# A two-layer attention trunk: the per-head factors of its output stages go through DRAM rows instead of TensorE turns, and the first tile is split by halves

## The chip, the core and the metric

The kernel runs on one core of a Trainium2 chip. The metric is the time of one execution on the device in microseconds; the time of a kernel is the median of its runs. The traces are of one profiled execution each.

## The reference, cut to what matters

```python
# per layer: attention heads o (SEQ x D), gate g, output projection, residual, norm
mixed = jnp.concatenate([a_out * jax.nn.silu(ag), b_out * jax.nn.silu(bg)], axis=-1)   # layer 0
y = mixed @ w_out_even[i]
...
y = (c_out * jax.nn.silu(cg)) @ w_out_odd[i]                                            # layer 1
...
x = x + y
return rms_norm(x, final_g)
```

SEQ is 2048, D is 1024, everything is float32. The attention outputs are left without their softmax denominators (heads of B and C) and without their RMS factor (heads of A). So an output stage computes, for each token and channel, `o * g * f`, where the factor `f` depends only on the token and on the head that the channel belongs to; then it multiplies by the output weights, adds the residual and norms.

## The kernel before, in words

There are two output stages, one per layer, both written by `output()` (L2144). The first ("stage 0") follows `small_attn` and precedes the projection of layer 1; the second ("stage 1") follows `band_attn` and is the end of the program. Each stage handles 16 tiles of 128 tokens. Everything is laid out with channels on the partitions: 8 chunks of 128 channels (two heads of 64 channels each; in stage 0 the first 4 chunks are one A head each) by 128 tokens.

For tile t:

- POOL *widens* (L1593, L1594): the factors lie with tokens on the partitions and one column per head. POOL copies each column over the channels of its head, into `post_wide`. Tiles 0 and 1 are widened at the end of the attention stage, tiles 2 to 15 inside the output stage, each as soon as its buffer of two is free.
- TensorE *spreads* (`spreads(t)`, L2294): 16 transposes of 64x128 turn `post_wide` so that channels are on the partitions, into PSUM `spread`.
- VectorE *splits* (`split(t)`): `gated = g * spread` (L2254), `mix = o * gated` (L2257); ScalarE rounds `m_hi = mix` (L2223); VectorE forms `m_lo = mix - m_hi` (L2259).
- TensorE multiplies (L2309): for each half of 512 output columns, 8 chunks by three products (hi by hi, lo by hi, hi by lo), 48 matmuls of 128x512 per tile.
- VectorE adds the residual per half (`y`, L2275); ScalarE squares and sums (L2232) and takes the root (L2234); VectorE forms the inverse with one step of refinement (L79 to L82, L2277, L2279) and writes `n` (L2281).
- SyncE issues the loads and stores: x of tile t+2 (L2194) once y of tile t is done, the y store (L2208, stage 0 only), the n store (L2210), and, at tiles 0, 4 and 8, the next block of 512 tokens of o and g, 2 MB each (L2189). The first block is loaded tile by tile during the attention stage (L1588, 512 KB each in runs of 512 bytes). All of these use one queue. (The loads of q and k in the first attention stage, L1260 to L1262 in `diff_attn`, go to 64 partitions each, in runs of 2 KB; around 640 us they are what the DMA engines carry.)

The order on TensorE is written out: `spreads(0)`; then for each t: `spreads(t+1)`, wait for `m_lo` of t, 48 matmuls. On VectorE it is `split(0)`, a wait for the gain vector, then for each t: `split(t+1)`, y of t in two halves, norm of t. Two buffers exist for `post_wide`, `m_hi`, `m_lo`, x, y and n, and four PSUM banks for the accumulators, so y of tile t waits for the y and n stores of tile t-2.

Of the kernel before, what the change touches and what calls it, by code (L numbers as in the profile page):

```python
# [20 lines left out]
F32 = mybir.dt.float32  # L21
F32R = mybir.dt.float32r
ALU = mybir.AluOpType
ACT = mybir.ActivationFunctionType
AX = mybir.AxisListType

P = 128
SEQ, D = 2048, 1024
KC = D // P
TILES = SEQ // P  # L30
BLK = 512
NBLK = SEQ // BLK
TPB = BLK // P
HD = 64
EPS = 1e-6
SCALE = HD ** -0.5
A_HEADS, B_HEADS, B_GROUP, C_HEADS = 4, 8, 4, 16
# [7 lines left out]
ROW = 384  # L45
# [2098 lines left out]
def output(nc, before, name, keep, scr, x_dram, w_hi, w_lo, y_dram, norm_dram, gain_dram, post, rms=None, after=None):  # L2144


    with ExitStack() as ctx:
        st = Stage(nc, ctx, name, before)
        o_sb, g_sb = post.o, post.g
        m_hi = st.sb("m_hi", [P, 2, KC, P], F32R)  # L2150
        m_lo = st.sb("m_lo", [P, 2, KC, P], F32R)
        gated, mix = st.sb("gated", [P, KC, P]), st.sb("mix", [P, KC, P])
        x_sb = st.sb("x", [P, 2, D])
        y_sb = st.sb("y", [P, 2, D])
        n_sb = st.sb("n", [P, 2, D])
        gain = st.sb("gain", [P, D])
        ssq, mean, root, inv = (st.sb(x, [P, TILES]) for x in ("ssq", "mean", "root", "inv"))
        acc = [st.ps(f"acc{i}", [P, BLK]) for i in range(4)]
        junk = st.ps("junk", [P, D])
        spread = st.ps("spread", [P, 2, KC * HD])  # L2160
        spread_tokens = spread[:, :, :].rearrange("p r (c t) -> p c r t", t=HD)
        spread_done, scaled = (st.sem(x) for x in ("spread_done", "scaled"))
        gain_loaded = st.sem("gain_loaded")
        blk_loaded, x_loaded, y_stored, n_stored = (st.sems(x, 2) for x in ("blk_loaded", "x_loaded", "y_stored", "n_stored"))
        mixed, hi_done, lo_done, mm_done, y_done = (st.sem(x) for x in ("mixed", "hi_done", "lo_done", "mm_done", "y_done"))
        sq_done, mean_done, root_done, inv_done, normed = (st.sem(x) for x in ("sq_done", "mean_done", "root_done", "inv_done", "normed"))
        ot = scr["ot"].rearrange("(c p) t -> p c t", p=P)
        gt = scr["gt"].rearrange("(c p) t -> p c t", p=P)
        x_v, y_v, n_v = (None if d is None else d.rearrange("(t p) d -> t p d", p=P) for d in (x_dram, y_dram, norm_dram))
        block = ctx.enter_context(nc.Block())  # L2170

        @block.gpsimd
        def _(pool):
            st.clear_before(pool)
            if after is not None:
                after.load_weights(pool)
            for t in range(2, TILES):
                pool.wait_ge(spread_done, t - 1)
                post.widen(t, rms)

        @block.sync
        def _(sp):
            def load_block(b):
                if b >= 2:
                    sp.wait_ge(mixed, TPB * (b - 1))
                    sp.wait_ge(lo_done, TPB * (b - 1))
                sp.wait_ge(post.stored[b], 16 * (post.heads // 2))
                for buf, part in ((o_sb, ot), (g_sb, gt)):
                    sp.dma_start(buf[b % 2][:, :, :], part[:, :, b * BLK:(b + 1) * BLK]).then_inc(blk_loaded[b % 2], 16)  # L2189

            def load_x(t):
                if t >= 2:
                    sp.wait_ge(y_done, 2 * (t - 1))
                sp.dma_start(x_sb[:, t % 2, :], x_v[t]).then_inc(x_loaded[t % 2], 16)  # L2194

            load_x(0)
            load_x(1)
            sp.dma_start(gain[:, :], gain_dram.partition_broadcast(P)).then_inc(gain_loaded, 16)
            for t in range(TILES):
                if t + 2 < TILES:  # L2200
                    load_x(t + 2)
                if t == 0:
                    load_block(1)
                elif t % TPB == 0 and t // TPB + 1 < NBLK:
                    load_block(t // TPB + 1)
                if y_v is not None:
                    sp.wait_ge(y_done, 2 * (t + 1))
                    sp.dma_start(y_v[t], y_sb[:, t % 2, :]).then_inc(y_stored[t % 2], 16)  # L2208
                sp.wait_ge(normed, t + 1)
                sp.dma_start(n_v[t], n_sb[:, t % 2, :]).then_inc(n_stored[t % 2], 16)  # L2210
                if after is not None and t == TPB + 2:
                    sp.wait_ge(n_stored[0], 16 * (TPB // 2 + 1))
                    after.load_tiles(sp, n_v)
            for s in n_stored + (y_stored if y_v is not None else []):
                sp.wait_ge(s, 16 * TILES // 2)

        @block.scalar
        def _(act):
            def hi(t):
                act.wait_ge(mixed, t + 1)  # L2220
                if t >= 2:
                    act.wait_ge(mm_done, 2 * (t - 1))
                nc.scalar.activation(m_hi[:, t % 2, :, :], mix[:, :, :], ACT.Copy).then_inc(hi_done, 1)  # L2223

            hi(0)
            for t in range(TILES):
                if t + 1 < TILES:
                    hi(t + 1)
                act.wait_ge(y_done, 2 * (t + 1))
                if t >= 1:  # L2230
                    act.wait_ge(sq_done, t)
                nc.scalar.activation(junk[:, :], y_sb[:, t % 2, :], ACT.Square, accum_out=ssq[:, t:t + 1]).then_inc(sq_done, 1)  # L2232
                act.wait_ge(mean_done, t + 1)
                nc.scalar.activation(root[:, t:t + 1], mean[:, t:t + 1], ACT.Sqrt).then_inc(root_done, 1)  # L2234

        @block.vector
        def _(dve):
# [8 lines left out]
            def split(t):  # L2246
                b = t // TPB
                if b == 0:
                    dve.wait_ge(post.tile_loaded[t], 32)
                elif t % TPB == 0:  # L2250
                    dve.wait_ge(blk_loaded[b % 2], 32 * ((b + 1) // 2))
                tokens = slice(t % TPB * P, (t % TPB + 1) * P)
                dve.wait_ge(spread_done, t + 1)
                nc.vector.tensor_tensor(gated[:, :, :].rearrange("p c (r t) -> p c r t", t=HD), g_sb[b % 2][:, :, tokens].rearrange("p c (r t) -> p c r t", t=HD),  # L2254
                                        spread_tokens, ALU.mult).then_inc(scaled, 1)
                dve.wait_ge(scaled, t + 1)
                nc.vector.tensor_tensor(mix[:, :, :], o_sb[b % 2][:, :, tokens], gated[:, :, :], ALU.mult).then_inc(mixed, 1)  # L2257
                dve.wait_ge(hi_done, t + 1)
                nc.vector.tensor_tensor(m_lo[:, t % 2, :, :], mix[:, :, :], m_hi[:, t % 2, :, :].bitcast(F32), ALU.subtract).then_inc(lo_done, 1)  # L2259

            split(0)
            dve.wait_ge(gain_loaded, 16)
# [21 lines left out]
        @block.tensor  # L2284
        def _(pe):
            def spreads(t):

                if t >= 1:
                    pe.wait_ge(scaled, t)
                pe.wait_ge(post.widened, (t + 1) * (2 if post.earlier else 1))  # L2290
                for c in range(KC):
                    for r in range(2):
                        rows = slice(r * HD, (r + 1) * HD)
                        last = nc.tensor.transpose(spread[:, r, c * HD:(c + 1) * HD], post.wide[rows, t % 2, c, :], keep["ident"][rows, rows])  # L2294
                last.then_inc(spread_done, 1)

            spreads(0)
            for t in range(TILES):
                if t + 1 < TILES:
                    spreads(t + 1)  # L2300
                pe.wait_ge(lo_done, t + 1)
                for half in range(2):
                    u = 2 * t + half
                    if u >= 4:
                        pe.wait_ge(y_done, u - 3)
                    step = 0
                    for c in range(KC):
                        for mt, wt in ((m_hi, w_hi), (m_lo, w_hi), (m_hi, w_lo)):
                            last = nc.tensor.matmul(acc[u % 4][:, :], mt[:, t % 2, c, :], wt[:, c, half * BLK:(half + 1) * BLK],  # L2309
                                                    start=step == 0, stop=step == 3 * KC - 1)  # L2310
                            step += 1
                    last.then_inc(mm_done, 1)
# [10 lines left out]
def trunk(nc, src, out):  # L2323
# [1 line left out]
        ("qh", (2 * C_W, SEQ), F32), ("ql", (2 * C_W, SEQ), F32), ("gt", (D, SEQ), F32), ("ot", (D, SEQ), F32),  # L2325
        ("v0_a", (SEQ, A_W), F32), ("v0_b", (B_KV // HD, P, TILES, HD), F32), ("v1", (C_HEADS, P, TILES, HD), F32), ("x1", (SEQ, D), F32), ("xn", (SEQ, D), F32),
        ("row_a", (A_HEADS, REL), F32), ("row_b", (B_HEADS, REL), F32), ("row_c", (C_HEADS, REL), F32),
        ("skew_a", (A_HEADS, P, ROW), F32), ("skew_b", (B_HEADS, P, ROW), F32), ("skew_c", (C_HEADS, P, ROW), F32))}
    with ExitStack() as ctx:
        keep = {name: ctx.enter_context(nc.sbuf_tensor(f"keep_{name}", shape, F32)) for name, shape in (  # L2330
            ("ident", [P, P]), ("sink", [P, B_HEADS]), ("sub_g", [P, 1]), ("nlam", [P, 1]))}

        w_loaded = [ctx.enter_context(nc.semaphore(f"w_loaded{i}")) for i in range(6)]
        x, norm_g = src["x"][0], src["norm_g"]
# [59 lines left out]
```

## Time and profile before

| | us |
|---|---|
| median of 3 runs | 2559.77 (2558.9 to 2565.64) |
| the profiled execution's own time | 2567.35 |
| its span | 2565.5 |
| stage 0, from the first spread to the last n store | about 1079 to 1282 |
| stage 1, the same | about 2363 to 2565.5 |

The span is what the trace covers; the execution's own time is 1.85 us more. Busy time of TensorE is the share of time with a matmul under way; matmuls are pipelined, so the interval between starts (about 0.23 us for a 128x512 one at the full clock) is shorter than the duration of one (0.39 us).

### The profile page before, as it was taken

Reading aid. Unit: us, or ns where it says so; the run is one execution under the profiler, and the core shown is the slowest. Engines: PE = TensorE matmul, PEld = TensorE weight load, DVE = VectorE, ACT = ScalarE, POOL = GpSimd, SP = SyncE. Lnnn points to the kernel's source line nnn. Section 1 sums busy time; section 2 is a strip of 40 time slices with the busy share of each in tenths; the row PEclk is TensorE's granted clock in tenths of the full one; section 3 lists DMA queues with packets and bytes.
Section 4 is the critical chain, followed back from the end, with each engine's and each line's share of the span. In section 5 each row is a group of like instructions: output and inputs, shape, how many; then the busy total and the mean of one; then the engine's idle time right before and its main releaser. Section 6 shows DMA issues by size and latency. Waiting matters only on the chain. (4 is left out here: it accounts for less than half of the span.)

```text
span 2565.5 us, 46268 instructions
## 1 busy us (share of the span) xinstructions
PE 2377.9 (93%) x17864; PEld 1976.7 (77%) x17864; DVE 1528.9 (60%) x2849; ACT 1137.0 (44%) x2401; POOL 1072.4 (42%) x852
## 2 busy tenths in 40 slices
PE   5999999997999998799879999899997999998998
PEld 4777778875888877688768888788885888887887
DVE  6444565334988897855554423744223888887555
ACT  4333343333777776622143333433332666665221
POOL 6687758772000002401068877678774201000000
PEclk9999999998999999899989999999998999999999
DMA  3555434456663234757334444345434453533452
GB/s 130 169 177 177 152 118 149 148 176 149 136 145 88 63 115 132 215 199 261 131 130 158 160 126 141 99 156 170 126 103 146 147 178 129 189 130 112 165 196 83
DMA packets 220745, 376.76 MB, mean 147 GB/s; under 512 B 54980, under 2 KB 108912, under 8 KB 219504
## 3 DMA queue, kind: packets, MB, share of 16 engines
q1 hardware_dynamic: 199376, 296.21, 36.4%
q0 software_dynamic: 19792, 75.50, 10.0%
q8 instruction: 144, 2.36, 0.4%
q10 hardware_dynamic: 1360, 2.10, 0.2%
q14 instruction: 73, 0.60, 0.1%
HBM read 236.33 MB, written 142.90 MB: 148 GB/s over the span
## 5 line engine op out<-in xcount | busy, mean ns | idle before, releaser
L1092 PE MATMUL p_acc<-p_operands,p_w_hi 128*128 128x512 f32 x1600 | 613.5, 394 | 5.1 <-DVE p_full_out L959 4.9
L310 POOL TENSOR_TENSOR p_w_lo<-p_w_raw,p_w_hi 128x512 fp32r<-128x512 f32 x240 | 332.8, 1395 | 153.1 <-ACT p_w_hi L573 152.8
L1092 PE MATMUL p_acc<-share,p_w_hi 128*128 128x512 f32 x1024 | 385.2, 396 | 12.5 <-DVE p_operands L735 6.1
L1092 PEld LDWEIGHTS p_acc<-p_operands,p_w_hi 128*128 128x128 f32 x1600 | 303.6, 190 | 67.1 <-POOL p_w_raw L328 4.7
L1092 PE MATMUL p_acc<-share,p_w_lo 128*128 128x512 f32 x896 | 351.2, 392 | 0.0
L573 ACT ACTIVATE p_w_hi<-p_w_raw 128x512 fp32r<-128x512 f32 x252 | 156.5, 624 | 244.8 <-POOL p_w_raw L328 113.8
L1092 PE MATMUL p_acc<-share_low,p_w_hi 128*128 128x512 f32 x624 | 250.4, 401 | 12.5 <-DVE p_operands L735 6.1
L1092 PE MATMUL p_acc<-share_low,p_w_lo 128*128 128x512 f32 x624 | 246.1, 394 | 0.0
L1092 PEld LDWEIGHTS p_acc<-share,p_w_hi 128*128 128x128 f32 x1024 | 192.8, 189 | 54.9 <-DVE p_operands L735 8.9
L865 DVE SCALAR_TENSOR_TENSOR p_lo_out<-p_full_out,p_hi_out 128x512 fp32r<-128x512 f32 x116 | 123.1, 1061 | 180.3 <-ACT p_hi_out L590 180.3
L1850 DVE CUSTOM_DVE_ANT_0 c_prob<-c_logits,c_bias 128x640 f32<-128x640 f32 (+4 forms) x256 | 179.5, 738 | 68.8 <-PE c_logits L1783 52.6
L1877 ACT ACTIVATE c_prob<-c_prob,c_neg_max 128x640 f32<-128x640 f32 (+4 forms) x256 | 193.2, 757 | 43.4 <-DVE c_neg_max L1850 43.4
L2309 PE MATMUL o_acc<-w_out_hi,o_m_hi 128*128 128x512 f32 x512 | 204.1, 399 | 6.4 <-DVE o_m_lo L2259 6.4
L2309 PE MATMUL o_acc<-w_out_hi,o_m_lo 128*128 128x512 f32 x512 | 200.9, 392 | 0.0
L2309 PE MATMUL o_acc<-w_out_lo,o_m_hi 128*128 128x512 f32 x512 | 200.8, 392 | 0.0
L1092 PEld LDWEIGHTS p_acc<-share,p_w_lo 128*128 128x128 f32 x896 | 169.1, 189 | 35.9
L1464 ACT ACTIVATE a_prob<-a_prob,a_neg_max 128x128 f32<-128x128 f32 (+15 forms) x128 | 153.5, 1200 | 62.2 <-DVE a_neg_max L1421 61.8
L310 POOL TENSOR_TENSOR p_w_lo<-ready_w,p_w_hi 128x512 fp32r<-128x512 f32 x96 | 132.3, 1387 | 102.0 <-ACT p_w_hi L573 101.8
L1783 PE MATMUL c_logits<-share 64*128 64x256 f32 (+2 forms) x1440 | 138.9, 324 | 29.8 <-DVE c_neg_max L1850 21.4
L945 DVE COPY p_full_out<-p_acc 128x512 f32<-128x512 f32 x56 | 38.7, 691 | 196.2 <-PE p_acc L1092 196.2
L1783 PEld LDWEIGHTS c_logits<-share 64*128 64x128 f32 x1440 | 112.6, 190 | 54.1 <-DVE c_neg_max L1850 38.4
L1827 PE MATMUL c_o<-c_prob_t,c_v 128*64 128x128 f32 x2240 | 151.7, 279 | 2.0 <-issue 1.9
(285 smaller groups left out, 4743.7 us busy)
## 6 DMA issues: line engine op xcount, KB each, us to landing
scr_qh<-p_hi_out SPq DMA_DIRECT2D x116, 256.0 KB, 2.5
scr_ql<-p_lo_out SPq DMA_DIRECT2D x116, 256.0 KB, 2.8
p_w_raw<-in_w_in_even POOLq DMA_DIRECT2D x26, 1024.0 KB, 7.5
scr_gt<-p_hi_out SPq DMA_DIRECT2D x128, 128.0 KB, 2.1
ready_w<-in_w_in_odd POOLq DMA_DIRECT2D x16, 1024.0 KB, 6.9
p_w_raw<-in_w_in_odd POOLq DMA_DIRECT2D x16, 1024.0 KB, 6.9
share<-scr_qh SPq DMA_DIRECT2D x28, 512.0 KB, 8.3
share<-scr_ql SPq DMA_DIRECT2D x28, 512.0 KB, 9.6
```

What stands on the lines that cost most here:

```text
L310: nc.gpsimd.tensor_tensor(w_lo[:, k, :, :], w_source(e, k), w_hi[:, k, :, :].bitcast(F32), ALU.subtract).then_inc(w_made, 1)
L573: nc.scalar.activation(w_hi[:, k, :, :], w_source(e, k), ACT.Copy).then_inc(w_cast, 1)
L865: nc.vector.scalar_tensor_tensor(out=lo_out[:, buf, :], in0=full_out[:, buf, :], scalar=factor, in1=hi_out[:, buf, :].bitcast(F32), op0=AL ...
L945: nc.vector.tensor_copy(full_out[:, n % 2, :], x[:, :]).then_inc(taken, 1)
L1092: last = nc.tensor.matmul(bank[:, :], wt[:, k, c, :], at[k][:, c, :], start=starts and step == 0, stop=step == 3 * HK - 1, skip_group_chec ...
L1464: nc.scalar.activation(p, p, ACT.Exp, bias=neg_max[:, j:j + 1], scale=-1.0, accum_out=row_sum[:, g % 2, m:m + 1]).then_inc(exp_done, 1)
L1783: last = nc.tensor.matmul(logits[half][:, lo:hi], q_sb[b][x][rows, i * P:(i + 1) * P], k_sb[b][y][rows, tile * P:tile * P + hi - lo], star ...
L1827: last = nc.tensor.matmul(o_ps[half * HD:(half + 1) * HD, at:at + P], v, prob_t[:, s % 2, t, half, :], start=t == 0, stop=t == w - 1)
L1850: nc.vector.tensor_tensor_reduce(out=prob[:, j, 0:n], in0=logits[half][:, END - n:END], in1=bias[:, b, WIDE - n:WIDE], scale=1.0, scalar=H ...
L1877: nc.scalar.activation(p, p, ACT.Exp, bias=neg_max[:, j:j + 1], scale=-1.0, accum_out=sums[:, 2 * hp + half, i:i + 1]).then_inc(exp_done, 1)
L2309: last = nc.tensor.matmul(acc[u % 4][:, :], mt[:, t % 2, c, :], wt[:, c, half * BLK:(half + 1) * BLK], start=step == 0, stop=step == 3 * K ...
```

## The change

It does four things, in both stages.

1. POOL no longer widens tiles 2 to 15, and TensorE no longer spreads them. Only tiles 0 and 1 still go that way.
2. TensorE turns the factors of all heads and tiles once (`turn_inverses`, two 128x128 transposes into the PSUM of `junk`, behind `spreads(0)`), ScalarE copies them to SBUF (`inv_t`), and SyncE stores them as rows of 128 tokens in a new DRAM array `scr_inv` and waits for that. For tiles 2 to 15 SyncE then loads `post_wide` from there with each row repeated over its 64 channels (128 in the case of an A head): three DMAs a tile in stage 0 and two in stage 1, 512 KB a tile in 1024 runs of 512 bytes. Tiles 2 and 3 are loaded at the start, tile t+3 in iteration t, behind x of t+2 and ahead of the block load and the stores.
3. `gated` of tiles 2 to 15 is a product of two SBUF operands.
4. Tile 0 is split by halves of four chunks: gate, mix, second gate, m_lo of the first half, then the second half. TensorE's first matmuls wait only for the first half. The counters are shifted by one for all later tiles (`after_tile`).

```diff
@@ output(), gpsimd
-            for t in range(2, TILES):
-                pool.wait_ge(spread_done, t - 1)
-                post.widen(t, rms)
@@ output(), sync
+            def store_inverses():
+                sp.wait_ge(inv_copied, len(invs))
+                for n, (source, first, heads) in enumerate(invs):
+                    sp.dma_start(inv_rows[n * P:n * P + heads * TILES, :], inv_t[0:heads * TILES, n, :]).then_inc(inv_stored, 16)
+                sp.wait_ge(inv_stored, 16 * len(invs))
+
+            def load_wide(t):
+                if t < 2 * SPREADS:
+                    sp.wait_ge(spread_done, t - 1)
+                else:
+                    sp.wait_ge(scaled, after_tile(t - 2))
+                for r in range(2):
+                    rows = bass.AP(tensor=inv_rows.tensor, offset=inv_rows.offset + (r * TILES + t) * P, ap=[[0, HD], [2 * TILES * P, KC - rest], [1, P]])
+                    sp.dma_start(post.wide[r * HD:(r + 1) * HD, t % 2, rest:KC, :], rows).then_inc(wide_loaded[t % 2], 16)
+                if rest:
+                    rows = bass.AP(tensor=inv_rows.tensor, offset=inv_rows.offset + (P + t) * P, ap=[[0, P], [TILES * P, rest], [1, P]])
+                    sp.dma_start(post.wide[:, t % 2, 0:rest, :], rows).then_inc(wide_loaded[t % 2], 16)
...
+            store_inverses()
+            for t in range(SPREADS, 2 * SPREADS):
+                load_wide(t)
             for t in range(TILES):
                 if t + 2 < TILES:
                     load_x(t + 2)
+                if 2 * SPREADS <= t + 3 < TILES:
+                    load_wide(t + 3)
@@ output(), scalar
-            hi(0)
+            high(0)
+            for n, (source, first, heads) in enumerate(invs):
+                act.wait_ge(inv_turned, n + 1)
+                nc.scalar.activation(inv_t[0:heads * TILES, n, :], junk[0:heads * TILES, n * BLK:n * BLK + P], ACT.Copy).then_inc(inv_copied, 1)
@@ output(), vector, split(t)
+                if t < SPREADS:
+                    dve.wait_ge(spread_done, t + 1)
+                else:
+                    dve.wait_ge(wide_loaded[t % 2], 16 * WIDE_LOADS * (t // 2))
...
+                gate(0)
+                mixture(0)
+                if t == 0:
+                    gate(1)
+                low(0)
+                if t == 0:
+                    mixture(1)
+                    low(1)
@@ output(), tensor
             spreads(0)
+            turn_inverses()
             for t in range(TILES):
-                if t + 1 < TILES:
+                if t + 1 < SPREADS:
                     spreads(t + 1)
-                pe.wait_ge(lo_done, t + 1)
+                if t >= 1:
+                    pe.wait_ge(lo_done, after_tile(t))
...
+                        if t == 0 and half == 0 and c in (0, KC // 2):
+                            pe.wait_ge(lo_done, 1 if c == 0 else 2)
```

## Rows read from the trace of the kernel before

**Rows 1.** The page: busy time, share of the span and instructions of each engine.
```profile
PE 2377.9 (93%) x17864; PEld 1976.7 (77%) x17864; DVE 1528.9 (60%) x2849; ACT 1137.0 (44%) x2401; POOL 1072.4 (42%) x852
```

**Rows 2.** Groups by line, stage 0: busy us, mean ns of one, idle before and releaser.
```profile
L2309 PE MATMUL o_acc<-w_out_hi,o_m_hi 128*128 128x512 f32 x256 | 102.0, 398 | 3.5 <-DVE o_m_lo L2259 3.5
```

**Rows 3.** Timeline of SyncE's DMA issues, stage 0: start us, us, what.
```profile
1100.10 0.33 SPq L2194 DMA_DIRECT2D o_x<-in_x  x1
...
1252.81 0.33 SPq L2194 DMA_DIRECT2D o_x<-in_x  x1
...
1264.56 0.32 SPq L2208 DMA_DIRECT2D scr_x<-o_y  x1
...
1275.43 0.32 SPq L2208 DMA_DIRECT2D scr_x<-o_y  x1
```

**Rows 4.** The same timeline, stage 1.
```profile
2383.26 0.32 SPq L2194 DMA_DIRECT2D o_x<-scr_x  x1
...
2535.97 0.32 SPq L2194 DMA_DIRECT2D o_x<-scr_x  x1
```

**Rows 5.** Timeline of VectorE, tiles 1 to 3 of stage 0.
```profile
1111.13 0.69 DVE L2275 TENSOR_TENSOR o_y<-o_acc,o_x 128x512 f32<-128x512 f32 x1 [1.82 <-PE o_acc L2309]
...
1116.88 1.22 DVE L2257 TENSOR_TENSOR o_mix<-share_low,o_gated 128x1024 f32<-128x1024 f32 x1
1119.23 1.22 DVE L2259 TENSOR_TENSOR o_m_lo<-o_mix,o_m_hi 128x1024 fp32r<-128x1024 f32 x1 [1.13 <-ACT o_m_hi L2223]
```

**Rows 6.** Timeline of all engines, start of stage 0.
```profile
1073.11 0.60 ACT L2129 ACTIVATE b_o_out<-b_o 128x512 f32<-128x512 f32 x1 [1.12 <-PE b_o L2052]
...
1080.54 1.22 DVE L2254 TENSOR_TENSOR o_gated<-share_low,o_spread 128x1024 f32<-128x1024 f32 x1 [4.67 <-PE o_spread L2294]
...
1081.79 1.88 DVE L2257 TENSOR_TENSOR o_mix<-share_low,o_gated 128x1024 f32<-128x1024 f32 x1
...
1081.82 1.12 PE L2294 MATMUL o_spread<-keep_ident,post_wide 64*128 64x64 f32 x16 [1.38 <-DVE o_gated L2254]
...
1082.51 1.63 POOL L1594 COPY post_wide<-post_inv_sums 128x512 f32<-128x512 f32 x1
...
1086.38 0.80 PE L2309 MATMUL o_acc<-w_out_hi,o_m_hi 128*128 128x512 f32 x1 [3.45 <-DVE o_m_lo L2259]
...
1090.32 0.39 PE L2309 MATMUL o_acc<-w_out_hi,o_m_hi 128*128 128x512 f32 x1
...
1091.82 1.23 DVE L2259 TENSOR_TENSOR o_m_lo<-o_mix,o_m_hi 128x1024 fp32r<-128x1024 f32 x1 [1.13 <-ACT o_m_hi L2223]
```

**Rows 7.** Timelines of VectorE and TensorE, start of stage 1.
```profile
2363.97 1.22 DVE L2254 TENSOR_TENSOR o_gated<-share,o_spread 128x1024 f32<-128x1024 f32 x1 [4.79 <-PE o_spread L2294]
...
2369.32 0.79 PE L2309 MATMUL o_acc<-w_out_hi,o_m_hi 128*128 128x512 f32 x1 [2.96 <-DVE o_m_lo L2259]
```

**Rows 8.** Windows: length, PE, PEld, DVE, ACT, POOL busy; granted clock, DMA share, GB/s.
```profile
647.00:648.00 1.00, 1.00 (x11) 1.00 (x10) 0.93 (x3) 1.00 (x2) 0.00 (x0) 1.00 1.05 207
1075.00:1076.00 1.00, 0.00 (x0) 0.00 (x0) 0.86 (x1) 0.00 (x0) 0.00 (x0) 1.00 1.21 291
1086.00:1087.00 1.00, 0.62 (x2) 0.53 (x3) 0.33 (x1) 0.00 (x0) 0.00 (x0) 0.50 0.87 315
1151.00:1152.00 1.00, 1.00 (x6) 0.83 (x5) 1.00 (x1) 0.00 (x0) 0.00 (x0) 1.00 1.04 406
```

**Rows 9.** DMA issues (windows 1060:1082, 1152:1154): KB each, us from issue to landing.
```profile
share_low<-scr_ot SPq DMA_DIRECT2D x4, 512.0 KB, 8.4
...
scr_xn<-o_n SPq DMA_DIRECT2D x1, 512.0 KB, 12.7
```

**Rows 10.** Timelines of SyncE and VectorE, tiles 4 to 6 of stage 0.
```profile
1146.37 0.69 DVE L2275 TENSOR_TENSOR o_y<-o_acc,o_x 128x512 f32<-128x512 f32 x1 [1.82 <-PE o_acc L2309]
...
1152.87 0.53 SPq L2210 DMA_DIRECT2D scr_xn<-o_n  x1
...
1167.36 0.68 DVE L2275 TENSOR_TENSOR o_y<-o_acc,o_x 128x512 f32<-128x512 f32 x1
```

More of the change, by code:

```diff
@@ L2152, in output @@
         gated, mix = st.sb("gated", [P, KC, P]), st.sb("mix", [P, KC, P])
+        inv_t = st.sb("inv_t", [P, 2, P])
         x_sb = st.sb("x", [P, 2, D])
@@ L2162, in output @@
         spread_done, scaled = (st.sem(x) for x in ("spread_done", "scaled"))
+        inv_turned, inv_copied, inv_stored = (st.sem(x) for x in ("inv_turned", "inv_copied", "inv_stored"))
+        wide_loaded = st.sems("wide_loaded", 2)
         gain_loaded = st.sem("gain_loaded")
@@ L2168, in output, with pieces, after_tile @@
         gt = scr["gt"].rearrange("(c p) t -> p c t", p=P)
+        inv_rows = scr["inv"]
         x_v, y_v, n_v = (None if d is None else d.rearrange("(t p) d -> t p d", p=P) for d in (x_dram, y_dram, norm_dram))
+        SPREADS = 2
+        rest = post.earlier
+        invs = [(post.inv_sums, min(post.heads, P // TILES) * h, min(post.heads, P // TILES)) for h in range(post.heads * TILES // P)]
+        if rest:
+            invs.append((rms, 0, rest))
+        WIDE_LOADS = 3 if rest else 2
+        HALVES = ((0, KC // 2), (KC // 2, KC))
+        def pieces(t):
+            return HALVES if t == 0 else ((0, KC),)
+        def after_tile(t):
+            return t + 2
         block = ctx.enter_context(nc.Block())
@@ L2176, in _ @@
                 after.load_weights(pool)
-            for t in range(2, TILES):
-                pool.wait_ge(spread_done, t - 1)
-                post.widen(t, rms)
         @block.sync
         def _(sp):
+            def store_inverses():
[11 more added lines that the diff above has]
+                    sp.dma_start(post.wide[r * HD:(r + 1) * HD, t % 2, rest:KC, :], rows).then_inc(wide_loaded[t % 2], 16)
+                if rest:
+                    rows = bass.AP(tensor=inv_rows.tensor, offset=inv_rows.offset + (P + t) * P, ap=[[0, P], [TILES * P, rest], [1, P]])
+                    sp.dma_start(post.wide[:, t % 2, 0:rest, :], rows).then_inc(wide_loaded[t % 2], 16)
             def load_block(b):
                 if b >= 2:
-                    sp.wait_ge(mixed, TPB * (b - 1))
-                    sp.wait_ge(lo_done, TPB * (b - 1))
+                    sp.wait_ge(mixed, after_tile(TPB * (b - 1) - 1))
+                    sp.wait_ge(lo_done, after_tile(TPB * (b - 1) - 1))
                 sp.wait_ge(post.stored[b], 16 * (post.heads // 2))
@@ L2218, in _, with high @@
         def _(act):
-            def hi(t):
-                act.wait_ge(mixed, t + 1)
+            def high(t):
                 if t >= 2:
                     act.wait_ge(mm_done, 2 * (t - 1))
-                nc.scalar.activation(m_hi[:, t % 2, :, :], mix[:, :, :], ACT.Copy).then_inc(hi_done, 1)
-            hi(0)
+                for n, (lo, hi) in enumerate(pieces(t)):
+                    act.wait_ge(mixed, n + 1 if t == 0 else after_tile(t))
+                    nc.scalar.activation(m_hi[:, t % 2, lo:hi, :], mix[:, lo:hi, :], ACT.Copy).then_inc(hi_done, 1)
+            high(0)
+            for n, (source, first, heads) in enumerate(invs):
+                act.wait_ge(inv_turned, n + 1)
+                nc.scalar.activation(inv_t[0:heads * TILES, n, :], junk[0:heads * TILES, n * BLK:n * BLK + P], ACT.Copy).then_inc(inv_copied, 1)
             for t in range(TILES):
                 if t + 1 < TILES:
-                    hi(t + 1)
+                    high(t + 1)
                 act.wait_ge(y_done, 2 * (t + 1))
@@ L2252, in split, with gate, mixture, low @@
                 tokens = slice(t % TPB * P, (t % TPB + 1) * P)
[L2253 to L2259, printed above, removed]
+                if t < SPREADS:
+                    dve.wait_ge(spread_done, t + 1)
+                else:
+                    dve.wait_ge(wide_loaded[t % 2], 16 * WIDE_LOADS * (t // 2))
+                first = 1 if t == 0 else after_tile(t)
+                def gate(n):
+                    lo, hi = pieces(t)[n]
+                    if t < SPREADS:
+                        nc.vector.tensor_tensor(gated[:, lo:hi, :].rearrange("p c (r t) -> p c r t", t=HD), g_sb[b % 2][:, lo:hi, tokens].rearrange("p c (r t) -> p c r t", t=HD),
+                                                spread_tokens[:, lo:hi], ALU.mult).then_inc(scaled, 1)
+                    else:
+                        nc.vector.tensor_tensor(gated[:, lo:hi, :], g_sb[b % 2][:, lo:hi, tokens], post.wide[:, t % 2, lo:hi, :], ALU.mult).then_inc(scaled, 1)
+                def mixture(n):
+                    lo, hi = pieces(t)[n]
+                    dve.wait_ge(scaled, first + n)
+                    nc.vector.tensor_tensor(mix[:, lo:hi, :], o_sb[b % 2][:, lo:hi, tokens], gated[:, lo:hi, :], ALU.mult).then_inc(mixed, 1)
+                def low(n):
+                    lo, hi = pieces(t)[n]
+                    dve.wait_ge(hi_done, first + n)
+                    nc.vector.tensor_tensor(m_lo[:, t % 2, lo:hi, :], mix[:, lo:hi, :], m_hi[:, t % 2, lo:hi, :].bitcast(F32), ALU.subtract).then_inc(lo_done, 1)
+                gate(0)
[6 more added lines that the diff above has]
+                    low(1)
             split(0)
@@ L2288, in spreads @@
                 if t >= 1:
-                    pe.wait_ge(scaled, t)
+                    pe.wait_ge(scaled, after_tile(t - 1))
                 pe.wait_ge(post.widened, (t + 1) * (2 if post.earlier else 1))
@@ L2295, in spreads, with turn_inverses @@
                 last.then_inc(spread_done, 1)
+            def turn_inverses():
+                for n, (source, first, heads) in enumerate(invs):
+                    nc.tensor.transpose(junk[0:heads * TILES, n * BLK:n * BLK + P], source[:, first:first + heads, :].rearrange("p h t -> p (h t)"),
+                                        keep["ident"][:, :]).then_inc(inv_turned, 1)
             spreads(0)
+            turn_inverses()
             for t in range(TILES):
-                if t + 1 < TILES:
+                if t + 1 < SPREADS:
                     spreads(t + 1)
-                pe.wait_ge(lo_done, t + 1)
+                if t >= 1:
+                    pe.wait_ge(lo_done, after_tile(t))
                 for half in range(2):
@@ L2327, in trunk @@
         ("row_a", (A_HEADS, REL), F32), ("row_b", (B_HEADS, REL), F32), ("row_c", (C_HEADS, REL), F32),
-        ("skew_a", (A_HEADS, P, ROW), F32), ("skew_b", (B_HEADS, P, ROW), F32), ("skew_c", (C_HEADS, P, ROW), F32))}
+        ("inv", (2 * P, P), F32), ("skew_a", (A_HEADS, P, ROW), F32), ("skew_b", (B_HEADS, P, ROW), F32), ("skew_c", (C_HEADS, P, ROW), F32))}
     with ExitStack() as ctx:
```

## The prediction, made before the changed kernel ran

> **What bounds the kernel now.** I read the page first: TensorE has a matmul under way in 93% of the span [rows 1]. Matmuls are pipelined, so that alone proves little. What matters is who waits for whom inside the two output stages, the only places that the change touches. The groups of stage 0 answer that: the 256 products that open each chunk waited for `m_lo` 3.5 us in all, in a stage of 202 [rows 2], and that was the first one of the stage [rows 6]. The timelines give the beat. From the x load that follows tile 0 to the one that follows tile 13 it is 1252.81 - 1100.10 = 152.71 us for 13 tiles, 11.747 each [rows 3]; in stage 1 (2535.97 - 2383.26)/13 = 11.747 [rows 4]. The last tile is the only one in front of which no spread is left, and it takes 1275.43 - 1264.56 = 10.87 us [rows 3]. So a spread costs 0.877 us of TensorE's own time, and nothing covers it.
>
> **Removed spreads.** Each stage loses the spreads of tiles 2 to 15, 14 of them: 14 x 0.877 = 12.3 us, 24.6 for both. That gain holds only if no other engine needs more than 10.87 us per tile, which is the next step.
>
> **VectorE as the next bound.** The loop is: second y half of tile t, square, root, norm, then gate, mix, m_hi, m_lo of t+2. It begins at 1111.13 and m_lo ends at 1119.23 + 1.22 = 1120.45, so 9.32 us [rows 5]. The matmuls of t+2 start one beat after that y half, less some 0.1 us: 10.8. Slack: 1.4 us. The gate now reads two SBUF operands, as the mix does, 1.22 against 1.21 us: cost 0.01, inside the slack [rows 5, 6]. POOL's widening goes: its queue is empty after the weight load, and it was never waited for by TensorE in the steady beat. Gain 0, and its use of the port shows only at the start (below).
>
> **The wide loads.** 512 KB a tile in 512-byte runs. Such runs move 291 GB/s to 128 partitions, large ones 406; loads to 64 partitions with 2 KB runs move only 207, with the DMA engines full [rows 8]. The new loads to 64 partitions have both handicaps. Their bounds: 524 KB/207 = 2.5 us at best, and, if the handicaps multiply, 207 x 291/406 = 148 GB/s, 3.5 us. I take 3.5 in stage 1. In stage 0 half of the bytes go to 128 partitions (262 KB/291 = 0.9) and half to 64 (262/148 = 1.8): 2.7 us. This lies beside the matmuls. Lead: issued about 1 us after the y of tile t, due at the gate of t+3, which follows the norm of t+1, 10.87 + 4.5 us after that y: 14.4 us. A landing of a 512 KB load of 512-byte runs took 8.4 us with four to eight in the queue [rows 9]. So 6 us are left, and the cost is 0. The "SBUF — State Buffer" page of the Trainium skill (Door 1, the DMA port swizzle) speaks against the change here: a transfer to partitions 0 to 63 reaches half of the ports and gets about half of the rate. The 207 GB/s agree with it [rows 8]. By the page's 218 GB/s a wide load takes about 2.4 us (an estimate), and the sum stays as it is.
>
> **The backlog behind a block load.** This is where the cover is thin. Tile 4 of stage 0: its second y half stands at 1146.37, its n store is issued at 1152.87 behind x, 4 MB of o and g and the y store, and lands 12.7 us later, at 1165.6, so 19.2 after the y [rows 9, 10]. The first y half of tile 6 reuses those buffers; it ran at 1167.36, 21.0 after [rows 10]. After the change it is due at 10.87 + 9.3 = 20.2, and n lands 2.7 later, at 21.9 (wide of tile 7 stands ahead of the block). VectorE waits 1.7 us and has the first half done at 22.6; the second is due at 21.7. 0.9 us late is inside the slack of 1.4: cost 0 on TensorE. The next wide load sits behind all this: x of tile 7 landed at about 20.4, now 23.1, wide of tile 8 at 25.8, due at 26.2. This happens for tiles 4 and 8 (no wide load stands ahead of the first block), and only in stage 0: stage 1 has no y store. The bounds: 0, and 2 to 3 us for each of the two, if the backlog is 4 us longer than I work out. I take 0.
>
> **The trip through DRAM at the start.** Turns, ScalarE's two copies (0.6 us is a 128x512 one [rows 6]) and the store follow the first split, at about 1085. From there: a store at the slow landing of 12.7 us or a few, then 8.4 [rows 9]. The gate of tile 2 is due 4.5 us after the y of tile 0, at about 1101. It is ready at 1093 if the store took nothing, at 1106 at worst, and then costs 5 - 1.4 = 3.6 us. I take 0, since at that time the queue holds x and gain and no blocks. SyncE waits meanwhile, but its next item, x of tile 2, is due only after y of tile 0. The DMA issues add perhaps 1.5 us a tile on SyncE (it blocked 4.25 us at the fullest), which has 10.87.
>
> **The first tile by halves.** Before: gate 1080.54, mix 1.88 (beside POOL's copy; 1.22 without it), m_hi, m_lo, first matmul 1086.38 [rows 5, 6]. A half of a VectorE operation is 0.69 [rows 5]. After: gate A, mix A, gate B end at 1080.54 + 3 x 0.69 = 1082.6. Then spread 1 runs on TensorE, 1.12 us [rows 6], since it waits for both gates, and stands ahead of the first matmul: 1083.7. m_hi A (0.6) and m_lo A (0.69) end at 1083.3, so the spread is what ends last. Gain 1086.4 - 1083.7 = 2.7. The second half's m_lo ends by about 1085.5, when TensorE has done four of its first 12 matmuls: no wait. Stage 1: gate at 2363.97, first matmul 2369.32 [rows 7]; 2363.97 + 2.07 + 1.12 = 2367.2, gain 2.1. The turns fall into TensorE's idle time: 0. Tile 1's m_lo ended at 1093.05 [rows 6] and is needed at about 1096: 0. Sum 4.8; bounds 2 (the semaphore trips of twice as many operations) and 6.
>
> **The clock.** At the start the granted clock is 0.50, that is 1.2 GHz [rows 8]; it follows a stretch in which TensorE had little to do. Matmuls ran slowly from 1086.38 until 1090.32 [rows 6], nine of them at 0.43 us instead of 0.227, 1.8 us lost per stage. Afterwards TensorE works without a break from 1082.6 on, the spread included. If the slow stretch is as long as before, counted from there, it ends at 1086.5, and only 2.8 us of matmuls are slow: 0.5 us gained per stage, 1.0 in all. If it rises when it did before, 15 matmuls are slow, 1.2 lost per stage. The range takes -1.2 to +1.8 for each. The Trainium skill ("TensorE: Matmul & The Clock Gate", Part 1) says that the slow phase is a time and not a number of matmuls, and that its end varies between runs; no row here decides that for the new start. By it the gain of 1.0 could as well be 0.
>
> **Sum.** 24.6 + 4.8 + 1.0 = 30.4 us. Against the profiled execution's own 2567.35: 2537.0. That execution is 7.6 us above the median of 2559.77; the gain does not depend on where it was lost, so I forecast 2559.8 - 30.4 = 2529.4 for the median.
>
> **The rivals.**
>
> *The backlog of stage 0 reaches TensorE* (chance 0.12). The blocks hold the queue nearly full, and DMA margins of half a microsecond to 2 us are thin. Against it: VectorE was never late there before. Price: three events of some 3 us, the start included: 2538.
>
> *VectorE becomes the bound* (0.05). If the gate with both operands in SBUF, beside three more DMAs, or the longer chain of semaphores adds 2 us per tile, the beat is 11.5 instead of 10.87 and the gain shrinks by 28 x 0.6 = 17: 2546. The mix speaks against it: it is of that form and takes 1.22.
>
> *The wide loads come late on every tile: slower than before* (0.04). A landing of L us sets the beat to half of (1 + L + 5): issue, landing, then gate to m_lo, over two tiles. It passes 10.87 at L = 16, and the old 11.75 at L = 17.5. With repeated reads of the same rows at, say, a tenth of 207 GB/s, L is about 25 and the beat 15.5: 28 x 3.75 = 105 us more, 2630. For it speaks only that no row shows so many reads of one row; the gain vector, read 128 times, is one case, and it landed among the others.
>
> *The change does not shorten what it removes* (0.03). If the 0.877 us were the wait of the last `m_lo` and not the spread, the beat would stay, and only the start gain: 2554. The last tile's 10.87 speaks against it [rows 3].
>
> **How the numbers follow.** A measurement of this kernel tells about 0.3% from nothing, 7.7 us: below 2552.1 is faster. Forecast 0.76. Faster: 0.76 + 0.12 + 0.05 = 0.93, less a little for the unknown, 0.92; same 0.04; slower 0.04. The range is 2529.4 less 5 (clock and start at their best, and 2 for the runs) to 2542, which takes in the backlog: 2524 to 2542.
>
> **What would show it.** Right: the beat of both stages is 10.87 to 10.9, TensorE without idle from the first matmul on, o_spread down from 512 transposes to 64, the first matmul 3.2 us after the gate begins (5.8 before). Wrong: VectorE's gate waiting for `scr_inv` DMAs, y waiting for the n store at tile 6 or 10 by more than 2 us, m_lo ahead of TensorE's idle time, a low clock beyond 1090.

## The result, and the profile after

The changed kernel takes 2657.66 us (median of 4 runs, 2655.23 to 2666.51) against 2561.88 before: ratio 1.0383, interval 1.0367 to 1.04. It is 96 us slower, where 30 us faster was forecast. Its profiled execution has a span of 2653.4 us.

The spreads of tiles 2 to 15 are gone (64 transposes are left of 512), and TensorE now waits. The groups of stage 0 after the change answer to [rows 2], those of stage 1 follow: busy us, mean ns, idle before and releaser.

```profile
L2386 PE MATMUL o_acc<-w_out_hi,o_m_hi 128*128 128x512 f32 x256 | 107.2, 419 | 52.3 <-DVE o_m_lo L2318 52.3
...
L2386 PE MATMUL o_acc<-w_out_hi,o_m_hi 128*128 128x512 f32 x256 | 106.2, 415 | 41.8 <-DVE o_m_lo L2318 41.8
```

3.5 us of waiting for `m_lo` in stage 0 have become 52.3, and 41.8 in stage 1. VectorE is not the slow one; it waits too. Its waits after, over the whole span: us in all, times, longest.

```profile
DVE o_gated L2308 <- DMA post_wide<-scr_inv: 82.9, 26, 6.5
...
DVE o_y L2343 <- DMA scr_xn<-o_n: 28.9, 3, 10.2
DVE o_y L2343 <- DMA out<-o_n: 25.2, 3, 10.2
```

The gate waits for the wide loads in 26 of 28 tiles; and three times a stage, at the tile that comes two after a block load, the first y half waits up to 10.2 us for the n store. The DMA issues say why: KB each, median us from issue to landing.

```profile
post_wide<-scr_inv SPq DMA_DIRECT2D x42, 256.0 KB, 16.8
o_x<-in_x SPq DMA_DIRECT2D x16, 512.0 KB, 10.9
scr_x<-o_y SPq DMA_DIRECT2D x16, 512.0 KB, 17.6
scr_xn<-o_n SPq DMA_DIRECT2D x16, 512.0 KB, 13.4
```

Nothing that shares the queue with the wide loads is quick any more: loads of x took 4.3 us in stage 0 of the kernel before and take 10.9 now. The low rate is visible at the start of stage 0, when the wide loads of tiles 2 and 3 are alone in the queue. Each line is a window: its length, then the busy time of PE, PEld, DVE, ACT and POOL, the clock, DMA share and GB/s. The first is 1 us of these loads; the second is 1 us behind the first wait of TensorE for a wide load; the third is the whole stage.

```profile
1095.00:1096.00 1.00, 1.00 (x6) 0.81 (x6) 0.51 (x1) 0.00 (x0) 0.00 (x0) 1.00 0.87 38
1111.00:1112.00 1.00, 1.00 (x4) 0.81 (x3) 0.32 (x1) 0.65 (x1) 0.00 (x0) 0.50 1.50 74
1079.00:1333.00 254.00, 192.88 (x788) 154.28 (x786) 114.88 (x195) 39.10 (x67) 0.90 (x1) 0.88 0.70 191
```

38 GB/s (38 to 46 in the five full microseconds from 1092 to 1097, before x joins the queue), where [rows 8] had 291 for runs of 512 bytes and 207 for 64 partitions. The granted clock was 1.00 up to TensorE's wait of 3.85 us (which ended at 1110.17), and 0.50 behind it; over the stage it was 0.88 on average, against 0.96 before.

### The profile page after: what moved, and what is told of

Its sections match the earlier page's. It is cut to its first block and busy times, and to the rows that moved or that the text cites. A ratio compares the mean times of both kernels' runs of the same rounds, so it can differ in the third digit from the quotient of the medians.

```text
span 2653.4 us, 45403 instructions
## 1 busy us (share of the span) xinstructions
PE 2380.0 (90%) x17420; PEld 1977.2 (75%) x17420; DVE 1529.2 (58%) x2855; ACT 1137.8 (43%) x2407; POOL 1040.1 (39%) x810
## 5 line engine op out<-in xcount | busy, mean ns | idle before, releaser
L2386 PE MATMUL o_acc<-w_out_hi,o_m_hi 128*128 128x512 f32 x512 | 213.4, 417 | 94.1 <-DVE o_m_lo L2318 94.0
L2386 PE MATMUL o_acc<-w_out_hi,o_m_lo 128*128 128x512 f32 x512 | 208.9, 408 | 0.0
L2386 PE MATMUL o_acc<-w_out_lo,o_m_hi 128*128 128x512 f32 x512 | 208.3, 407 | 0.0
L2386 PEld LDWEIGHTS o_acc<-w_out_hi,o_m_hi 128*128 128x128 f32 x512 | 102.5, 200 | 124.1 <-DVE o_m_lo L2318 102.3
```

## The experiments

Two theories of the slow loads stood at first. **A**: reading one row of 512 bytes for all partitions queues at one place in DRAM; A1, at any distance between the rows of a load, or A2, only because these rows lie a power of two apart (16 KB between chunks, 8 KB for the A heads). **B**: 64 partitions by 512-byte runs are slow by themselves. A third says that the loads are not the whole loss and that another engine has become the bound.

**e1_no_wide.** The wide loads of tiles 4 to 15 are left out, which leaves those tiles with the factors of tiles 2 and 3.

```diff
-                if 2 * SPREADS <= t + 3 < TILES:
-                    load_wide(t + 3)
...
-                    dve.wait_ge(wide_loaded[t % 2], 16 * WIDE_LOADS * (t // 2))
+                    dve.wait_ge(wide_loaded[t % 2], 16 * WIDE_LOADS)
```

> Leaves out the wide loads of tiles 4 to 15 in both stages (those tiles are gated with the factors of tiles 2 and 3), keeps all else of the change. If the slow wide loads are the whole loss, the sum of the prediction holds: 24.6 us for the spreads and about 5 for the start, less some us that the four wide loads left still cost at tile 2: 2530 to 2542 us and a beat of 10.87 to 10.9. The rival that VectorE (a gate from two SBUF operands) or ScalarE is the new bound expects a beat over 11.2 and more than 2545.

Measured: 2564.58 us, ratio to before 1.0007 (0.9996 to 1.0017). The total missed the expectation by 22 us or more, the beat did not. From the x load of one tile to the next, late in stage 0:

```profile
1189.95 0.33 SPq L2228 DMA_DIRECT2D o_x<-in_x  x1
...
1255.23 0.33 SPq L2228 DMA_DIRECT2D o_x<-in_x  x1
```

10.88 us each over these six tiles, so no other engine is the bound: that theory falls. The loss is in the two tiles' loads that remain in each stage: they hold the queue, and behind them the first block lands late. That block load in e1 (the start of stage 0), and then the wait of y for the n store (all of stage 0):

```profile
share_low<-scr_ot SPq DMA_DIRECT2D x1, 2048.0 KB, 25.5
```

```profile
DVE o_y L2341 <- DMA scr_xn<-o_n: 9.7, 1, 9.7
```

It takes 25.5 us to land, where the median of the three such loads of stage 0 is 8.6. TensorE waits for `m_lo` 22.9 us in e1, in five waits near the starts of the two stages, and runs slowly behind the long ones. Wide loads for two tiles a stage thus use up all that the 28 removed spreads give.

**e2_distinct, e3_near, e5_pitch.** All three keep shape, run length and bytes of the wide loads and change the addresses alone. Only the stage's own term is shown, that of the A heads is changed likewise.

```diff
 change:      ap=[[0, HD],   [2 * TILES * P,         KC - rest], [1, P]]      # scr_inv
+e2_distinct: ap=[[SEQ, HD], [P * SEQ,               KC - rest], [1, P]]      # gate array
+e3_near:     ap=[[0, HD],   [2 * P,                 KC - rest], [1, P]]      # scr_inv
+e5_pitch:    ap=[[0, HD],   [2 * TILES * P + 2 * P, KC - rest], [1, P]]      # gate array
```

In all three, and in e9 to e11 below, the factors of tiles 2 to 15 are other numbers than the reference's.

> The wide loads keep their number, shape (64 or 128 partitions, 512-byte runs) and bytes, but every partition reads a row of its own of the gate array in DRAM instead of one row repeated (the factors are then wrong numbers). Theory A (all partitions read the same row at the same time, and one place in DRAM serves about 40 GB/s): loads land in under 9 us, 2530 to 2550 us. Theory B (64 partitions with 512-byte runs are slow by themselves, 148 GB/s at best): about as the change, 2640 to 2670.

> As the change, each row still repeated over its channels in 512-byte runs, but the rows that one load reads lie 1 KB apart (8 KB in all) instead of 8 or 16 KB apart. Theory A1 (one row at a time is the one place, whatever the distance): as the change, 2640 to 2670. Theory A2 (rows a power of two apart, 8 or 16 KB, fall on the same place, so that all reads of a load queue there): 2530 to 2560. In between if engines out of step spread over the neighbouring rows.

> As the change, rows repeated in 512-byte runs, read from the gate array (wrong numbers) at a distance of 17 KB (9 KB for the A heads) instead of 16 KB (8 KB). Theory A2 (power-of-two distance) expects the loads to be fast, 2530 to 2560 us. Theory A1 expects 2640 to 2670.

Measured: 2534.47, 2534.35 and 2535.02 us, one run each beside a before of 2561.73. All three are 27 us under before, and nearly the same. e2 rules out B: the shape is not what is slow. e3 and e5 rule out A1: the same repetition is fast when the rows lie 1 KB or 17 KB apart. A microsecond of the first wide loads of e2, then of e5, and the landings of e5:

```profile
1093.00:1094.00 1.00, 1.00 (x6) 0.84 (x5) 0.64 (x1) 0.00 (x0) 0.00 (x0) 1.00 0.95 238
```

```profile
1092.00:1093.00 1.00, 1.00 (x6) 0.84 (x5) 0.00 (x0) 0.00 (x0) 0.00 (x0) 1.00 1.05 283
```

```profile
post_wide<-scr_gt SPq DMA_DIRECT2D x42, 256.0 KB, 5.5
```

283 GB/s instead of 38, and 5.5 us instead of 16.8, from 1 KB more in a distance of 16. (e5 also reads another array, but so do e9 and e11 below, which are slower; e3 and e8 read `scr_inv` and are fast. The array doesn't decide it.) In e2 every row lies a multiple of 8 KB from every other one of its load (8 KB from partition to partition, 1 MB from chunk to chunk), and the load is fast: the power of two does no harm by itself there.

**e9_4k.** As e5, rows 4 KB apart: `ap=[[0, HD], [8 * P, KC - rest], [1, P]]`.

> Rows repeated as in the change, but 4 KB apart (both kinds of heads), read from the gate array (wrong numbers). Tells whether every power of two over 1 KB is slow or only 8 and 16 KB: slow (2600 or more) if the place in DRAM is chosen by bits below 4 KB, fast (2533 to 2540, as at 1 KB) if by the bits above, in between (2545 to 2600) if 4 KB leaves two or four places.

Measured: 2551.17 us beside 2561.82, in between, as it would be for a few places instead of one. At the start:

```profile
1090.00:1091.00 1.00, 1.00 (x6) 0.84 (x5) 0.00 (x0) 0.00 (x0) 0.00 (x0) 1.00 0.26 82
```

82 GB/s, twice the 38 (51 to 86 in the microseconds from 1086 to 1091).

**e10_own_rows, e11_one_row.** Distance and repetition taken apart. e10 keeps 16 KB between chunks and gives each partition rows of its own; e11 lets all chunks and partitions read one row.

```diff
+e10_own_rows: ap=[[P, HD], [2 * TILES * P, KC - rest], [1, P]]      # gate array
+e11_one_row:  ap=[[0, HD], [0,             KC - rest], [1, P]]      # gate array
```

> The chunks of a partition lie 16 KB apart as in the change (8 KB for the A heads), but every partition reads rows of its own, 512 bytes further than its neighbour's, from the gate array (wrong numbers). If the power-of-two distance is enough to make the loads slow, 2640 to 2670 us. If it needs the repetition too (all partitions at the same row), 2532 to 2540, loads landing in under 6 us.

> Every run of a load, all chunks and all partitions, reads one and the same row of 512 bytes (wrong numbers). If all reads of a load at one place in DRAM are what is slow, this is at least as slow as the change: 2640 us or more. If reading one row again and again is cheap and only different rows at the same place collide, it is fast, 2532 to 2545.

Measured: 2530.40 and 2662.57 us beside 2562.01. The distance alone does no harm (e10); one row for everything is as bad as the change (e11; the two can't be told apart). The first loads of e10, then of e11:

```profile
1094.00:1095.00 1.00, 1.00 (x6) 0.81 (x6) 0.51 (x1) 0.00 (x0) 0.00 (x0) 1.00 1.00 254
```

```profile
1093.00:1094.00 1.00, 1.00 (x6) 0.83 (x5) 0.10 (x1) 0.86 (x1) 0.00 (x0) 1.00 0.16 45
```

So what the change does with 8 different rows 16 KB apart (in stage 0 with 4 of them and 4 that lie 8 KB apart) costs the same as reading a single row. The reading that fits is that all partitions come to the same few hundred bytes at the same time, and that the next rows lie where the first one does; the place itself is inferred and was not observed. A2 stands, in the form "repeated, and 8 or 16 KB apart": the distance alone does no harm (e2, e10), the repetition alone none where the rows lie 1 or 17 KB apart (e3, e5), and 1 KB is a power of two as well, so it is not every power of two.

**e6_halves.** Part 4 of the change alone: all tiles widened by POOL and spread by TensorE, no factor in DRAM.

```diff
-        SPREADS = 2
+        SPREADS = TILES
...
+            for t in range(2, TILES):
+                pool.wait_ge(spread_done, t - 1)
+                post.widen(t, rms)
...
-            store_inverses()
-            for t in range(SPREADS, 2 * SPREADS):
-                load_wide(t)
...
-            turn_inverses()
```

> The split of the first tile by halves alone, on the kernel before: all 16 tiles are still widened by POOL and spread by TensorE, and no factor goes through DRAM. By the prediction's term for the halves: 2.7 and 2.1 us less POOL's copies beside the mix (which stay here and make VectorE's two SBUF operands slower), and up to 1 us of the clock: 2 to 6 us under before, 2555 to 2560. If a later wait takes it back (tile 1 waits for the gain vector), 0.

Measured: 2555.66 us beside 2561.82, ratio 0.9977 (0.9968 to 0.9987): 6.2 us, with an interval from 3 to 8.

**e7_ordered, e8_padded.** Two cures that keep all values. e7 has POOL reorder the factors on the tokens' side before the turn (into the dead `post_sums` and a small tile), so that the rows of one tile and half lie side by side, and a partition reads one run. e8 leaves one row of padding between heads.

```diff
+            for source, place, some in invs:                                  # e7, POOL
+                nc.gpsimd.tensor_copy(place, source).then_inc(inv_ordered, 1)
...
+e7: offset (2 * t + r) * own * P,        ap=[[0, HD], [P, own], [1, P]]
+e8: offset (r * (TILES + 1) + t) * P,    ap=[[0, HD], [2 * (TILES + 1) * P, KC - rest], [1, P]]
```

> The change with the rows kept in the order in which a tile reads them: POOL first reorders the factors on the tokens' side, so that the turned rows of one tile and one half of the partitions lie side by side; each partition then reads one run of 4 KB (2 KB in stage 0) instead of 8 rows 16 KB apart. Theory A2 (repeated rows at a power-of-two distance are slow) expects 2528 to 2535, at or a little under the 2534 of the runs with the distance changed, since runs are longer. If POOL's reordering or the store at the start delays tile 2, some us more.

> The smallest cure that keeps the values: the change with one row of padding between heads, so that the rows of a load lie 17 KB apart (8.5 KB for the A heads) instead of 16 (8); the factors are stored with one DMA per head. Theory A2 expects 2530 to 2540 (16 small stores cost SyncE about 5 us at the start, which tile 2 has). If only the distance of the test with the gate array mattered by accident (another array, other pages of DRAM), 2600 or more.

Measured: e7 2530.62 us, ratio to before 0.9884 (0.9861 to 0.9907); e8 2532.68, ratio 0.9891 (0.9874 to 0.9907). One of the four executions of e8 took 7365 us, for which no run has a reason; the ratio is that of the other three. e7 and e8 can't be told apart, and both beat both kernels. e7's matmuls, waits and beat in stage 0:

```profile
L2396 PE MATMUL o_acc<-w_out_hi,o_m_hi 128*128 128x512 f32 x256 | 100.5, 393 | 0.4 <-DVE o_m_lo L2328 0.3
```

```profile
DVE o_y L2353 <- DMA scr_xn<-o_n: 5.0, 2, 2.6
...
PE o_acc L2396 <- DVE o_m_lo L2328: 0.3, 1, 0.3
```

```profile
1116.55 0.33 SPq L2238 DMA_DIRECT2D o_x<-in_x  x1
...
1127.42 0.33 SPq L2238 DMA_DIRECT2D o_x<-in_x  x1
```

The gate waits for no wide load at all, and the beat is 10.87 away from the block loads. TensorE waits 0.3 us in 16 tiles; by the starts of its matmuls the two places behind block loads cost it 1.0 us.

## Why the prediction was wrong

**The step that failed** is the price in "The wide loads": 2.7 to 3.5 us for the 512 KB of a tile, from rates of 148 to 291 GB/s. Those rates came from rows whose reads are all different. The rate depends here on the addresses: 38 GB/s at the start, by which 524 KB take 13.8 us. That is more than the beat of 10.87, so the loads could not be hidden in any place. The cover was 14.4 us, and the landing was put at 8.4; the 256 KB loads landed after 16.8 us at the median, and the slowest wide load after 26.1. The loads were issued late as well. SyncE was to lose perhaps 1.5 us more a tile, and had been held for 4.25 at the fullest before; now the issue of one store behind the first block load held it for 11.8 us in stage 0 (from 1111.26) and 12.0 in stage 1 (from 2439.13).

**The case that came true** was one of the rivals for slower, "the wide loads come late on every tile", which had 0.04 and 2630 us; 2657.66 came. Its mechanism was right in the main (many reads of one row), but repetition alone is fast in e3 and e5, and its numbers agree by luck. The 2630 doesn't follow from its own sum: 105 us more than 2559.8, less the 5.8 of the start, is 2659. That this is close comes from two errors against each other. The rate was taken as 21 GB/s and was 38 to 46; and the beat was worked out from the landing alone, by which 16.8 us give (1 + 16.8 + 5)/2 = 11.4. The x loads stand 15.8 us apart in stage 0 (1097.34 to 1303.06, 13 tiles) and 15.0 in stage 1, because the issues came late, y waited for the n stores (54.1 us in six waits), and the clock fell. What misled me was the argument against it: the gain vector, read by 128 partitions, had landed in time. That row is 4 KB long, and e3 shows that repeated rows within 8 KB are fast. It was no instance of a 512-byte row that all partitions read together with others 16 KB off.

**The loss, put together.** TensorE waited 52.3 + 41.8 = 94.1 us for `m_lo`; the kernel with the loads cured (e7) waits 0.3. The spans differ by 2653.4 - 2528.1 = 125.3 us, so some 31 are left. Most of that is the clock: behind a long wait the granted clock is 0.50 (as from 1111 to 1112), and the matmuls start 0.43 us apart instead of 0.227. Counted from the starts of the output stages' matmuls (those that start 0.3 to 0.62 us after the one before, where 0.227 is the full clock), 135 of 1536 were slow after the change and lost 27.4 us, and 14 in e7, which lost 3.0. So some 24 of the 31 are the clock, and some 7 stay open.

**The terms that held**, as e6 and e7 show:
- *Removed spreads*: 24.6 us forecast; e6 to e7 is 2555.66 - 2530.62 = 25.0.
- *VectorE as the next bound*: beat 10.87 to 10.9 forecast, 10.88 in e1 and 10.87 in e7 away from the block loads; the gate from SBUF took 1.22 us as the mix does.
- *Halves and clock*: 4.8 + 1.0 forecast, 6.2 measured by e6. In the changed kernel the first matmul came 3.12 us after the gate began (1079.20 to 1082.32), 3.2 forecast; it was 5.84 before [rows 6]. In stage 1 it is 2412.49 to 2415.61, the same:

```profile
1079.20 0.69 DVE L2305 TENSOR_TENSOR o_gated<-share_low,o_spread 128x512 f32<-128x512 f32 x1 [5.38 <-PE o_spread L2362]
...
1082.32 0.79 PE L2386 MATMUL o_acc<-w_out_hi,o_m_hi 128*128 128x512 f32 x1
...
1086.66 0.40 PE L2386 MATMUL o_acc<-w_out_hi,o_m_lo 128*128 128x512 f32 x1
```

  The clock rose after ten slow matmuls here, after five in stage 1 of the same trace (2415.61 to 2417.84), and after six in e7 (1081.64 to 1084.34); it was nine before. The Trainium skill ("TensorE: Matmul & The Clock Gate", Part 1) says that its point varies between runs. These traces agree, so the 1.0 us of that term could have come out with either sign.
- *The sum*: -30.4 us forecast; e7 is 31 under its before of 2561.8, with an interval from 24 to 36, so the agreement to 1 us is in part luck. Of the terms of the sum one failed, and it was worth 127 us (2657.66 - 2530.62).
- *The backlog behind a block load*: with fast loads, y waits for the n store twice in stage 0, 2.6 us at most (e7); 1.7 was worked out for each, and that it would not reach TensorE. It reached it with 0.3 us of waiting. With slow loads y waits up to 10.2 us, in both stages and after the first block too; I had left stage 1 and the first block out, which is right only for fast loads.
- *The trip through DRAM at the start*: store issued at 1083.61, wide loads at 1090.58. That is in time when the loads are fast: e7 has 1082.94 and 1089.30, and its gate waits for none of them.

## What to carry to other kernels

A broadcast from DRAM is priced by its addresses before its bytes: if all partitions read the same short row at the same time, ask where the next row lies, and put the rows of one load side by side, in the order in which they are read (e7), or pad a distance of 8 or 16 KB by a row (e8). A rate taken from a load with different addresses bounds nothing for a repeated one; where no row of the trace has the pattern, the range has to reach to the case in which the load doesn't fit into the beat. And when a load sits in a queue that also carries stores, its slowness returns as waits on buffers that have nothing to do with it.

## What the runs showed of the hardware

- Loads of 512-byte rows, each repeated over 64 or 128 partitions, ran at 38 to 46 GB/s with rows 16 KB (8 KB) apart, 29 to 45 with a single row, 51 to 86 at 4 KB, 159 to 247 at 1 KB (e3) and 157 to 283 at 17 KB (e5): each the lowest and highest full microsecond at the start of stage 0 while these loads were alone. With rows of their own per partition it was 166 to 271 with 16 KB between chunks (e10) and 200 to 281 in e2. The four highest ranges can't be ranked by this. Times of the kernel: 2658, 2663, 2551, 2534, 2535, 2530 and 2534.
- A place in DRAM that serves some 40 GB/s and is chosen by address bits would explain the low rates; that mechanism is an inference. Bits below 16 KB alone don't do: in e2 all rows of a load agree in them but for one bit, and it is fast. Higher bits would have to count too, or the reads of one row at the same time matter for themselves; no run tells these apart.
- The Trainium skill ("DMA: Bandwidth & Descriptors", Latency and other measured facts) reports that copies slow down where rows lie 2 MiB or more apart in powers of two, and run at 207 GB/s at 512 KiB, near the full rate. Here 16 KB are enough, when the reads are repeated, and do nothing when they are not (e10).
- The busy share of the DMA engines says little about such loads: it was 0.20 at 44 GB/s and 0.87 at 38 within 3 us of the same loads (from 1092 and from 1095), and 0.12 to 0.16 with a single row (e11). Other transfers in the queue wait with them: x took 10.9 us to land.
- Four such tile loads (two a stage) cost the kernel 34 us (e1 against e7), although each overlaps with matmuls.
